# Hybrid decoder trunk: the value projection moved behind scores and softmax, the attention transposes moved inside the output projection

## The chip, the cores and the metric

One core of a Trainium2 chip runs the whole program, one launch. A core has five engines that this text names by their short names: PE (TensorE, matrix products and transposes), DVE (VectorE), ACT (ScalarE), POOL (GpSimd) and SP (SyncE, which here only issues the weight loads). They run side by side and wait for each other through semaphores; each takes its own instructions in order. The metric is the device time of one execution in microseconds (us); the smaller the better. The time before is 628.68 us, the median of 3 runs (627.68 to 630.69).

## The reference

Two layers over 256 tokens of width 1024, all in float32. Cut to what matters here (the mixture of experts behind it is not touched):

```python
for l in range(DEPTH):                                   # DEPTH = 2
    mod = (c_act @ w_ada[l] + b_ada[l])[:, None, :]      # 6 * 1024 wide
    shift1, scale1, gate1, shift2, scale2, gate2 = jnp.split(mod, 6, axis=-1)
    h = rmsnorm(x, norm1_g[l]) * (1.0 + scale1) + shift1
    u = h @ w_in[l]                                      # 1024 x 3072
    u_b, u_c, u_h, u_q, u_k, u_v = jnp.split(u, split_at, axis=-1)
    y_conv = u_b * conv3(u_c * u_h)                      # causal, depthwise, 3 taps
    q = rope(rmsnorm(heads(u_q), q_norm_g[l]), positions)
    k = rope(rmsnorm(heads(u_k), k_norm_g[l]), positions)
    v = heads(u_v)                                       # 8 heads of 64
    y_att = softmax(mask(q @ k.T * scale)) @ v           # one block of 256: plain causal
    y_mix = concat([rmsnorm(y_conv, conv_out_g[l]), rmsnorm(y_att, attn_out_g[l])])
    x = x + gate1 * (y_mix @ w_out[l])                   # 1024 x 1024
    h2 = rmsnorm(x, norm2_g[l]) * (1.0 + scale2) + shift2
    x = x + gate2 * hier_moe(h2, ...)                    # 16 experts, top 2 of one group
```

## The kernel before, in words

Tokens lie in T = 2 tiles of 128 (or, transposed, channels on the partitions and S = 256 tokens in the free dimension). The six blocks of 512 columns of `w_in` and the eight row tiles of `w_out` are multiplied in three passes: ACT writes the rounded weight into `whi` (line 490, `split_half` on ACT), DVE writes the rest `raw - whi` into `wlo` (line 758), and PE adds whi*act_hi, wlo*act_hi and whi*act_lo. A half is 1024 columns of such a pair. A layer has 32 halves: 0 to 11 are q, k and v (three blocks interleaved in two parts), 12 to 15, 16 to 19 and 20 to 23 the blocks B, C and h of the conv, 24 to 31 `w_out`. A half's slot is one of RING = 6, so ACT may not begin half n before PE has used half n-6 (`unit_used`).

Weights come in units of 1 MB into ten slots of `raw` through SP's queue, strictly in the order of the list `stream`: in a layer the 12 units of `w_in` (the first ones earlier), 8 units G (`w_ada` columns of the two gates), 4 units of `w_out`, 8 units M (`w_ada` columns of the second modulation), in layer 0 8 units A (the next layer's first modulation), then the experts. Each unit takes the slot of the unit ten places ahead of it in the list and waits until that one is used up: with the units of a layer's `w_in` and `w_out` counted w0 to w15, G7 waits until w9 (halves 18 and 19) is split, w12 and w13 (the first of `w_out`) until w10 and w11 (halves 20 to 23) are, and the last two of M until w12 and w13 (halves 24 to 27) are.

The order on every engine is written out by hand. In layer l PE does halves 0 to 11 (line 1291, by token), B and C (`conv_block`, line 1307, by channel), transposes q and k (line 1320), h, then attention: `scores` (1344) for pairs of heads u = 0 and 1, the first half of G (1206), `scores(2)`, `probs_T` (1352), the rest of G, `values` (1361 to 1363), and so on pair by pair; then the sum of squares of the conv output (1386), M (1206), the first four row tiles of `w_out` (1396), `ada_cols` (1229), the transposes of the attention rows (1412), and the last four row tiles. DVE squares and sums q and k for their norm (899, 901), applies rope (909 to 922), multiplies C by h (930), does `softmax_max` per pair (939, 944: scale and mask, then a maximum for each token tile), the three taps (972, 974), `heads_out` (953, 956), the conv output's norm (984 to 991) and the attention rows' norm (997 to 1004). ACT takes projections out of PSUM (567, 578, 585, 590, 596), does exp (606), `pT_out` (614) and the square of the conv output (628). POOL only brings the gate rows to all partitions.

PSUM has eight banks; the four pairs of heads use banks 0-1, 4-5, 2-3 and again 0-1 (`PAIR_BANK`), the scores in columns 0 to 383 and the values' result in columns 384 to 511 of the same bank.

## Time and profile before

| what | before |
|---|---|
| median of 3 runs | 628.68 us |
| profiled execution: its own time | 629.93 us |
| its span | 628.1 us |
| mean granted TensorE clock | 0.949 |
| PE busy | 553.2 us (88%) |
| DVE busy | 282.7 us (45%) |
| ACT busy | 218.8 us (35%) |
| bytes moved | 189.77 MB, mean 302 GB/s |

How to read it: the span is the time from the first to the last recorded instruction; the profiled execution took 1.83 us more around it and 1.25 us more than the median. PE is busy most of the time, so idle time of PE and stretches at a low granted clock are what can be gained or lost; the other engines count where PE waits for them. Line numbers (L1307) are those of the kernel before; in the changed kernel they differ by a few.

### The profile page before, as it was taken

What the parts mean: (1) busy time and instruction counts of PE and PEld (TensorE: products, weight loads), DVE (VectorE), ACT (ScalarE), POOL (GpSimd) and SP (SyncE); (2) the same over time, 40 slices, a digit from 0 to 9 for tenths busy, and PEclk for the clock granted to TensorE, in tenths of its full rate; (3) what the DMA queues carried; (4) which work ended last, traced back from release to release, by engine and by line L of the source; (5) the groups of instructions that cost most, each with busy time, mean ns of one, the idle gap of its engine ahead of it and who ended that gap; (6) DMA issues with size and microseconds to landing.
All of it is one profiled execution on the core that took longest, in us unless ns stands there. A gap on an engine that the chain in (4) does not pass through costs nothing.

```text
span 628.1 us, 7864 instructions
## 1 busy us (share of the span) xinstructions
PE 553.2 (88%) x3140; PEld 355.2 (57%) x3140; DVE 282.7 (45%) x495; ACT 218.8 (35%) x379; POOL 17.0 (3%) x74
## 2 busy tenths in 40 slices
PE   3797999869799999999949999986976899999993
PEld 1566899455656534444327899944664644444331
DVE  4516890964266022222377389196326502222233
ACT  2415533641044422221145453364105432232120
POOL 3004000000000000000000000000000000000000
PEclk9898999979798999999987999997978799999998
DMA  8999943891599999999997644299069089999951
GB/s 312 388 387 369 360 158 129 335 423 47 210 417 411 379 386 416 414 412 415 402 387 290 216 143 160 101 365 410 30 229 373 8 288 380 416 413 413 413 213 69
DMA packets 51726, 189.77 MB, mean 302 GB/s; under 512 B 4618, under 2 KB 4698, under 8 KB 44260
## 3 DMA queue, kind: packets, MB, share of 16 engines
q1 hardware_dynamic: 50464, 185.62, 75.9%
q0 software_dynamic: 896, 2.45, 1.1%
q10 hardware_dynamic: 324, 1.13, 0.5%
q8 instruction: 28, 0.46, 0.3%
q14 instruction: 14, 0.11, 0.0%
HBM read 188.12 MB, written 1.06 MB: 301 GB/s over the span
## 4 chain that ended last, share of the span: by engine, by line
PE 77%; DVE 13%; ACT 5%; issue 2%; DMA 1%; DVEq 0%; SPq 0%; ACTq 0%
PE ps L1492 18%; PE ps L1307 11%; PE ps L1291 11%; PE ps L1518 9%; PE ps L1396 6%; PE ps L1472 6%; PE ps L1532 5%; PE ps L1206 4%; DVE wlo L758 3%; PE ps L1237 1%; DMA raw<-in_w_ada_dram 1%; DVE cbc L974 1%; PE ps L1386 1%; ACT whi L490 1%; ACT work L606 1%
## 5 line engine op out<-in xcount | busy, mean ns | idle before, releaser
L758 DVE TENSOR_TENSOR wlo<-raw,whi 128x1024 fp32r<-128x1024 f32 x64 | 75.0, 1221 | 19.3 <-ACT whi L490 19.1
L490 ACT ACTIVATE whi<-raw 128x1024 fp32r<-128x1024 f32 x64 | 64.8, 1054 | 27.1 <-PE ps L1291 8.7
L1492 PE MATMUL ps<-raw,qkT 128*64 128x512 f32 x256 | 58.3, 597 | 1.6 <-ACT work L709 1.6
L1518 PE MATMUL ps<-raw,work 128*64 128x512 f32 x256 | 58.0, 598 | 0.0
L1492 PE MATMUL ps<-raw,cbc 128*64 128x512 f32 x256 | 57.2, 594 | 0.0
L1147 DVE SCALAR_TENSOR_TENSOR work<-ps,cw,work 128x256 f32<-128x256 f32 x16 | 10.9, 684 | 102.7 <-ACT work L703 102.7
L1206 PE MATMUL ps<-raw,c_rep 128*32 128x512 f32 x384 | 46.0, 616 | 10.8 <-DMA raw<-in_w_ada_dram 10.8
L1307 PE MATMUL ps<-act_hi,whi 128*128 128x256 f32 x192 | 54.5, 284 | 0.0
L1307 PE MATMUL ps<-act_hi,wlo 128*128 128x256 f32 x192 | 54.3, 283 | 0.0
L1307 PE MATMUL ps<-act_lo,whi 128*128 128x256 f32 x192 | 54.3, 283 | 0.0
L1136 DVE TENSOR_TENSOR v_sb<-ps,gates 128x512 f32<-128x512 f32 x32 | 22.1, 691 | 64.6 <-PE ps L1518 64.6
L1291 PE MATMUL ps<-whi,act_hi 128*128 128x512 f32 x96 | 39.9, 416 | 7.3 <-DVE act_lo L861 4.0
L1291 PE MATMUL ps<-whi,act_lo 128*128 128x512 f32 x96 | 39.3, 410 | 0.0
L1291 PE MATMUL ps<-wlo,act_hi 128*128 128x512 f32 x96 | 39.3, 409 | 0.0
L693 ACT ACTIVATE whi<-v_sb 128x512 fp32r<-128x512 f32 x32 | 20.0, 629 | 53.8 <-DVE v_sb L1136 45.4
L1472 PE MATMUL ps<-whi,act_hi 128*128 128x256 f32 x128 | 37.1, 319 | 0.9 <-DVE whi L1087 0.9
L1492 PEld LDWEIGHTS ps<-raw,cbc 128*64 128x64 f32 x256 | 18.0, 137 | 34.8 <-issue 33.7
L1472 PEld LDWEIGHTS ps<-whi,act_hi 128*128 128x128 f32 x128 | 26.4, 206 | 18.9 <-issue 18.9
L1307 PEld LDWEIGHTS ps<-act_hi,wlo 128*128 128x128 f32 x192 | 36.8, 192 | 0.1
L1307 PEld LDWEIGHTS ps<-act_hi,whi 128*128 128x128 f32 x192 | 36.8, 192 | 0.1
L1307 PEld LDWEIGHTS ps<-act_lo,whi 128*128 128x128 f32 x192 | 36.8, 192 | 0.0
L1492 PEld LDWEIGHTS ps<-raw,qkT 128*64 128x64 f32 x256 | 17.3, 137 | 33.1 <-issue 28.0
(227 smaller groups left out, 842.2 us busy)
## 6 DMA issues: line engine op xcount, KB each, us to landing
raw<-in_w_ada_dram SPq DMA_DIRECT2D x40, 1024.0 KB, 8.5
raw<-in_w_gate_dram SPq DMA_DIRECT2D x64, 512.0 KB, 7.6
raw<-in_w_up_dram SPq DMA_DIRECT2D x64, 512.0 KB, 9.5
raw<-in_w_down_dram SPq DMA_DIRECT2D x32, 1024.0 KB, 11.4
raw<-in_w_in_dram SPq DMA_DIRECT2D x24, 1024.0 KB, 14.5
raw<-in_w_ada_dram SPq DMA_DIRECT2D x16, 512.0 KB, 11.7
raw<-in_w_out_dram SPq DMA_DIRECT2D x8, 1024.0 KB, 5.2
gates<-gate_line POOLq DMA_DIRECT2D x2, 1024.0 KB, 6.4
```

The lines of the kernel that those rows point to most:

```text
L490: act.activation(whi[:, slot(n), :], raw[:, r, (i % 2) * 1024:(i % 2 + 1) * 1024], ACT.Copy).then_inc(hi_done, 1)
L693: act.activation(y_hi[:, cols], y_f[:, cols], ACT.Copy).then_inc(yhi_ready, 1)
L758: dve.tensor_tensor(wlo[:, slot(n), :], raw[:, ring_slot[("w", l, i // 2)], (i % 2) * 1024:(i % 2 + 1) * 1024], whi[:, slot(n), :].bitcast ...
L1136: dve.tensor_tensor(y_f[:, cols], ps[:, 2 + n, :], gates[:, 1, cols], ALU.mult).then_inc(yg_ready, 1)
L1206: ins = pe.matmul(ps[32 * i:32 * i + 32, 6, :], c_rep[:, row, :], raw[:, ring_slot[unit], i * 512:(i + 1) * 512], start=(k == 0), stop=(k ...
L1291: ins = pe.matmul(ps[:, bank + t, :], acts[pa][:, k, t * P:(t + 1) * P], w[pw][:, kk * 512:(kk + 1) * 512], start=(k == 0 and p == 0), sto ...
L1307: ins = pe.matmul(ps[:, bank + j // 2, (j % 2) * S:(j % 2 + 1) * S], w[pw][:, kk * 512 + j * P:kk * 512 + (j + 1) * P], acts[pa][:, k, :], ...
L1396: ins = pe.matmul(ps[:, 2 * t + n, :], acts[pa][:, k, t * P:(t + 1) * P], w[pw][:, n * 512:(n + 1) * 512], start=(k == 0 and p == 0), stop ...
L1472: ins = pe.matmul(ps[:, bank, j * S:(j + 1) * S], xn[part][:, t, k * P:(k + 1) * P], sel[:, t, 256 * q:256 * (q + 1)], start=(t == 0 and p ...
L1492: ins = pe.matmul(ps[i * SLOTS:(i + 1) * SLOTS, 0, :], hg[p // 2 % 2][:, k, c0:c0 + SLOTS], ws[i][:, :, kk, :], start=(k == 0), stop=(k == ...
L1518: ins = pe.matmul(ps[i * SLOTS:(i + 1) * SLOTS, 2 + n, :], hidT[:, p % 2, kk, i * SLOTS:(i + 1) * SLOTS], ws[i][:, c0:c0 + 512], start=(kk ...
L1532: ins = pe.matmul(ps[:, 4 + 2 * t + n, :], selT[:, 2 * p + t, :], ys[part][:, n * 512:(n + 1) * 512], start=(p == 0 and part == 0), stop=( ...
```

## The change

Nothing that is computed changes, only its order and where it lies.

- The blocks of `w_in` are taken in another order: q, k and B first (halves 0 to 11; B by channel), then C (12 to 15), h (16 to 19) and last v (20 to 23, by token). The list of loads is the same; only which columns a unit holds differs.
- `scores(0)` and `scores(1)` run before h instead of behind all of `w_in`, their softmax under h; `scores(2)` and `scores(3)` run before v, their softmax under v. `probs_T` stands before the last half of each block.
- All of G is accumulated by PE before the first scores, four units ahead of the q and k transposes and four behind them; DVE adds its bias (`gate_row`) before the first softmax.
- The values of all heads are computed in one go behind v, four heads to a bank (0 and 1); `heads_out` runs twice per layer instead of four times.
- q and k are squared and summed one after the other, each as soon as it is out of PSUM; the splits of single halves are spread between the steps.
- The attention rows are transposed behind the first of the eight row tiles of `w_out` instead of behind the fourth.

```diff
-PAIR_BANK = (0, 4, 2, 0)
+PAIR_BANK = (0, 2, 0, 2)
-    IN_ORDER = (3, 4, 5, 0, 1, 2)
+    IN_ORDER = (3, 4, 0, 1, 2, 5)
 # ACT
                 split(l, 10)
+                (qkT out of PSUM, from banks 0-1 and 2-3)
                 exps(0)
                 exps(1)
+                split(l, 11)
+                split_half(l, 24)
+                pT_out(0)
+                pT_out(1)
+                split_half(l, 25)
+                exps(2)
+                exps(3)
                 split(l, 13)
-                pT_out(0)
-                exps(2)
-                pT_out(1)
                 pT_out(2)
-                exps(3)
-                split(l, 14)
                 pT_out(3)
+                split_half(l, 28)
                 act.wait_ge(yconv_ready, l + 1)
                 act.activation(cb, cc, ACT.Square).then_inc(csq_ready, 1)
+                act.wait_ge(unit_used, n0 + 24)
+                act.activation(v_sb[:, :, :], ps[:, 4:6, :], ACT.Copy).then_inc(proj_evac, 1)
                 act.wait_ge(csum_done, l + 1)
...
 # DVE
+                def head_squares(w):
+                    dve.wait_ge(proj_evac, 5 * l + 1 + w)
+                    cols = slice(w * AW, (w + 1) * AW)
+                    squares = wflat[:, w * 1024:(w + 1) * 1024]
+                    link(dve.tensor_tensor(squares.rearrange("p (t d) -> p t d", t=T), tokmaj[:, :, cols],
+                                           tokmaj[:, :, cols], ALU.mult))
+                    dve.tensor_reduce(stat[:, 4:36].rearrange("p (t w h) -> p w t h", t=T, w=2)[:, w, :, :],
+                                      squares.rearrange("p (t h d) -> p t h d", t=T, d=HD),
+                                      AX.X, ALU.add).then_inc(qk_sum, 1)
+                head_squares(0)
                 split(l, 6)
+                head_squares(1)
                 split(l, 7)
-                split(l, 8)
...
-                def heads_out(u):
+                def heads_out(a):
+                    dve.wait_ge(pv_done, 2 * l + a + 1)
+                    dve.tensor_tensor(
+                        tokmaj[:, :, 256 * a:256 * (a + 1)].rearrange("p t (h d) -> p t h d", d=HD),
+                        ps[:, a, :].rearrange("p (h t d) -> p t h d", t=T, d=HD),
+                        stat[:, 20:36].rearrange("p (t h) -> p t h", t=T)[:, :, 4 * a:4 * a + 4].unsqueeze(3)
+                        .to_broadcast([P, T, 4, HD]), ALU.mult).then_inc(yatt_raw, 1)
+                gate_row(l)
                 softmax_max(0)
                 softmax_max(1)
+                split(l, 11)
+                dve.wait_ge(proj_evac, 5 * l + 4)
+                dve.wait_ge(unit_used, n0 + 20)
+                dve.tensor_tensor(cg[:, :, 2:S + 2], cc, ps[:, 4:6, :]..., ALU.mult).then_inc(gated_done, 1)
+                split(l, 12)
                 softmax_max(2)
-                split(l, 13)
+                softmax_max(3)
                 (the three taps, times cb: yconv_ready)
+                split(l, 13)
+                split_half(l, 28)
...
 # PE
+                pe.wait_ge(proj_evac, 5 * l + 1)
+                for half in range(4):
+                    in_half(12 + half, 4, 2 * half, True)
+                ada_acc("G", l, range(0, 4))
+                pe.wait_ge(rope_done, T * (l + 1))
+                qk_transposes(0)
+                qk_transposes(1)
+                ada_acc("G", l, range(4, 8))
                 pe.wait_ge(qkT_ready, 2 * l + 2)
                 scores(0)
                 scores(1)
-                ada_acc("G", l, range(0, 4))
-                pe.wait_ge(gated_done, l + 1)
-                scores(2)
+                pe.wait_ge(proj_evac, 5 * l + 4)
+                for half in range(3):
+                    in_half(16 + half, 4, 2 * half, True)
                 probs_T(0)
                 probs_T(1)
+                in_half(19, 4, 6, True)
+                pe.wait_ge(pT_ready, 4 * l + 1)
+                scores(2)
+                pe.wait_ge(pT_ready, 4 * l + 2)
+                scores(3)
+                pe.wait_ge(gated_done, l + 1)
+                for half in range(3):
+                    in_half(20 + half, 4, 2 * half, False)
+                probs_T(2)
+                probs_T(3)
+                in_half(23, 4, 6, False)
+                (sum of squares of the conv output, into bank 7)
+                pe.wait_ge(pT_ready, 4 * (l + 1))
+                pe.wait_ge(proj_evac, 5 * (l + 1))
                 values(0)
                 values(1)
                 ada_acc("M", l, range(0, 8))
...
                 for half in range(4):
                     for t in range(T):
                         ins = out_half(0, half, t, (0, 1))
                     ins.then_inc(unit_used, 1)
-                ada_cols("M", l)
-                pe.wait_ge(yatt_ready, l + 1)
-                (the 8 transposes of the attention rows)
+                    if half == 0:
+                        ada_cols("M", l)
+                        pe.wait_ge(yatt_ready, l + 1)
+                        (the 8 transposes of the attention rows)
```

How the instructions stand now. First PE around the first scores of layer 0. In the kernel before, the scores of the first two pairs (L1344) stand behind the last matmul of block h (L1307), and the first half of G (L1206, `ps<-raw,c_rep`) behind them:

```order
L1307 MATMUL ps<-act_lo,whi 128x256
L1344 MATMUL ps<-qkT 128x128
L1344 MATMUL ps<-qkT 128x256
L1344 MATMUL ps<-qkT 128x128
L1344 MATMUL ps<-qkT 128x256
L1344 MATMUL ps<-qkT 128x128
L1344 MATMUL ps<-qkT 128x256
L1344 MATMUL ps<-qkT 128x128
L1344 MATMUL ps<-qkT 128x256
L1206 MATMUL ps<-raw,c_rep 32x512 x16
L1344 MATMUL ps<-qkT 128x128
```

In the changed kernel both halves of G (L1208) stand ahead of the scores (L1333), one on each side of the q and k transposes (L1319), and block h begins behind the scores (L1283):

```order
L1208 MATMUL ps<-raw,c_rep 32x512 x16
L1319 MATMUL ps<-ident,tokmaj 128x128 x16
L1208 MATMUL ps<-raw,c_rep 32x512 x16
L1333 MATMUL ps<-qkT 128x128
L1333 MATMUL ps<-qkT 128x256
L1333 MATMUL ps<-qkT 128x128
L1333 MATMUL ps<-qkT 128x256
L1333 MATMUL ps<-qkT 128x128
L1333 MATMUL ps<-qkT 128x256
L1333 MATMUL ps<-qkT 128x128
L1333 MATMUL ps<-qkT 128x256
L1283 MATMUL ps<-act_hi,whi 128x256
```

Moved: the scores of two pairs went from behind block h to ahead of it, and both halves of G to ahead of them.

Second, DVE from the splits before rope to rope, layer 0. Before, both squares and one sum stand behind eight splits (L758), and four more splits stand ahead of rope (L906, L909):

```order
L758 TENSOR_TENSOR wlo<-raw,whi 128x1024 x8
L899 TENSOR_TENSOR work<-tokmaj 128x1024 x2
L901 TENSOR_REDUCE stat<-work 128x32
L758 TENSOR_TENSOR wlo<-raw,whi 128x1024 x4
L906 RECIPROCAL stat<-stat 128x32
L909 TENSOR_TENSOR tokmaj<-tokmaj,stat 128x1024
```

After, q's square and sum (L902, L904) come two splits earlier, and only two splits stand ahead of rope (L913, L916):

```order
L760 TENSOR_TENSOR wlo<-raw,whi 128x1024 x6
L902 TENSOR_TENSOR work<-tokmaj 128x1024
L904 TENSOR_REDUCE stat<-work 128x2x8
L760 TENSOR_TENSOR wlo<-raw,whi 128x1024 x2
L902 TENSOR_TENSOR work<-tokmaj 128x1024
L904 TENSOR_REDUCE stat<-work 128x2x8
L760 TENSOR_TENSOR wlo<-raw,whi 128x1024 x2
L913 RECIPROCAL stat<-stat 128x32
L916 TENSOR_TENSOR tokmaj<-tokmaj,stat 128x1024
```

Moved: q's square and sum went two splits up, and two splits went from ahead of rope to behind its first token tile.

Third, PE in the output projection, layer 0. Before, all four row tiles (L1396) stand ahead of `ada_cols` (L1229) and the attention transposes (L1412):

```order
L1396 MATMUL ps<-whi,act_hi 128x512 x2
L1396 MATMUL ps<-wlo,act_hi 128x512 x2
L1396 MATMUL ps<-whi,act_lo 128x512 x2
L1229 MATMUL ps<-rowsel,mod_rows 128x4 x4
L1412 MATMUL ps<-ident,tokmaj 128x128 x8
L1396 MATMUL ps<-whi,act_hi 128x512 x2
L1396 MATMUL ps<-wlo,act_hi 128x512 x2
```

After, these two (L1231, L1415) stand behind the first row tile, with three row tiles (L1398) behind them:

```order
L1398 MATMUL ps<-whi,act_hi 128x512 x2
L1398 MATMUL ps<-wlo,act_hi 128x512 x2
L1398 MATMUL ps<-whi,act_lo 128x512 x2
L1231 MATMUL ps<-rowsel,mod_rows 128x4 x4
L1415 MATMUL ps<-ident,tokmaj 128x128 x8
L1398 MATMUL ps<-whi,act_hi 128x512 x2
L1398 MATMUL ps<-wlo,act_hi 128x512 x2
```

Moved: 36 projection matmuls now stand between the transposes and the first matmul that needs their result.

## Rows read from the trace of the kernel before

**Rows 1.** Stretches: their length, busy us of PE, PEld, DVE, ACT, POOL, PEclk, DMA, GB/s
```profile
72.10:165.30 93.20, 81.01 (x608) 65.39 (x607) 59.38 (x91) 37.65 (x68) 1.13 (x2) 0.96 0.53 206
369.40:462.50 93.10, 80.81 (x609) 65.23 (x608) 59.46 (x91) 37.65 (x68) 1.13 (x2) 0.96 0.50 195
90.00:92.00 2.00, 2.00 (x19) 2.00 (x18) 2.00 (x2) 0.52 (x1) 0.00 (x0) 1.00 0.00 0
108.90:127.00 18.10, 15.28 (x137) 8.67 (x138) 16.60 (x28) 9.57 (x29) 0.00 (x0) 1.00 0.82 324
127.00:134.00 7.00, 2.73 (x22) 2.05 (x18) 6.83 (x15) 4.23 (x11) 0.56 (x1) 0.96 1.01 420
134.00:141.00 7.00, 5.79 (x24) 5.00 (x28) 2.43 (x2) 2.92 (x4) 0.56 (x1) 0.56 1.02 419
165.30:174.00 8.70, 8.67 (x27) 6.90 (x28) 0.19 (x1) 0.00 (x0) 0.00 (x0) 0.68 0.99 417
188.00:300.00 112.00, 109.35 (x578) 54.37 (x572) 30.03 (x69) 35.13 (x68) 1.05 (x2) 0.98 1.01 405
```

**Rows 2.** Chain of waits, layer 0, 72 to 182: start us, us, what
```profile
72.08 23.05 PE ps L1307 x192
...
135.22 3.78 PE ps L1386 x8
...
140.48 0.22 PE ps L1362 x2
...
140.93 7.00 PE ps L1206 x64
147.93 11.15 PE ps L1396 x48
159.08 1.65 PE ps L1229 x8
...
165.33 8.39 PE ps L1396 x24
```

**Rows 3.** Timeline of PE: start us, us, line, operation, count, idle before
```profile
108.76 1.69 PE L1344 MATMUL ps<-qkT 64*128 64x128 f32 x16
110.38 3.64 PE L1206 MATMUL ps<-raw,c_rep 128*32 128x512 f32 x32
...
116.29 0.88 PE L1352 MATMUL ps<-ident,work 128*128 128x128 f32 x6 [1.41 <-ACT work L606]
...
160.58 1.07 PE L1412 MATMUL ps<-ident,tokmaj 128*128 128x128 f32 x8
```

**Rows 4.** Timeline of DVE, layer 0
```profile
67.80 2.48 DVE L899 TENSOR_TENSOR work<-tokmaj 128x1024 f32<-128x1024 f32 x2 [2.13 <-ACT tokmaj L567]
70.32 2.29 DVE L901 TENSOR_REDUCE stat<-work 128x32 f32<-128x2048 f32 x1
72.52 4.62 DVE L758 TENSOR_TENSOR wlo<-raw,whi 128x1024 fp32r<-128x1024 f32 x4
...
89.96 4.63 DVE L758 TENSOR_TENSOR wlo<-raw,whi 128x1024 fp32r<-128x1024 f32 x4
...
112.35 0.95 DVE L939 SCALAR_TENSOR_TENSOR work<-ps,mask 128x768 f32<-128x768 f32 x1
113.33 1.01 DVE L944 TENSOR_REDUCE stat<-work 128x2 f32<-128x256 f32 x2
...
121.79 1.00 DVE L974 SCALAR_TENSOR_TENSOR cbc<-cg,mix_col,cbc 128x256 f32<-128x256 f32 x2
...
147.51 0.88 DVE L1004 TENSOR_SCALAR tokmaj<-tokmaj,stat 128x512 f32<-128x512 f32 x2
```

**Rows 5.** Timeline of ACT: the square of the conv output
```profile
134.12 1.05 ACT L628 ACTIVATE cbc<-cbc 128x1024 f32<-128x1024 f32 x1
```

**Rows 6.** Timeline of SP's queue, 80 to 93: the last gate unit
```profile
84.95 0.37 SPq L331 DMA_DIRECT2D raw<-in_w_ada_dram  x1
```

**Rows 7.** Page, part 6: DMA issues, KB each, us to landing
```profile
raw<-in_w_out_dram SPq DMA_DIRECT2D x8, 1024.0 KB, 5.2
```

More of the change, by code:

```diff
@@ L615, in pT_out @@
                                    ACT.Copy).then_inc(pT_ready, 1)
+                split(l, 4)
+                split(l, 5)
+                qk_out(0)
+                split(l, 6)
+                qk_out(1)
+                split(l, 7)
+                act.wait_ge(qk_sum, 2 * (l + 1))
+                act.activation(stat[:, 4:36], stat[:, 4:36], ACT.Sqrt, scale=1.0 / HD,
+                               bias=eps_col).then_inc(qk_root, 1)
+                act.wait_ge(unit_used, n0 + 12)
+                act.activation(cb, ps[:, 2:4, :].rearrange("p a (b s) -> p (a b) s", s=S),
+                               ACT.Copy).then_inc(proj_evac, 1)
@@ new lines, in _ @@
+                split(l, 8)
+                split(l, 9)
+                act.wait_ge(unit_used, n0 + 16)
+                act.activation(cc, ps[:, 4:6, :].rearrange("p a (b s) -> p (a b) s", s=S),
+                               ACT.Copy).then_inc(proj_evac, 1)
+                split(l, 10)
+                act.wait_ge(rw_ready, 1)
+                for w in range(2):
+                    act.wait_ge(qkT_done, 2 * l + w + 1)
+                    bank = (0, 2)[w]
+                    act.activation(qkT[:, w, :, :],
+                                   ps[:, bank:bank + 2, :].rearrange("p a (b s) -> p (a b) s", s=S),
+                                   ACT.Copy).then_inc(qkT_ready, 1)
@@ L992, in _ @@
                                   ALU.subtract).then_inc(ymc_ready, 1)
-                heads_out(3)
-                dve.wait_ge(yatt_raw, 4 * (l + 1))
+                for a in range(2):
+                    heads_out(a)
+                dve.wait_ge(yatt_raw, 2 * (l + 1))
                 for t in range(T):
```

196 lines of the change are left out of this document (63 added, 133 removed).

## The prediction

> **What bounds the kernel now.** I read the stretches first, then the chain of waits, then the timelines of single engines inside the stretch that the chain shows to be weak.
>
> The stretch that the change rewrites runs from the start of half 12 (72.1) to the start of the last four row tiles of `w_out` (165.3): 93.2 us in layer 0 and 93.1 in layer 1 [rows 1]. PE is busy for 81.0 of them, so 12.2 us per layer are waits, and part of the busy time is slow. The reader is to see two holes in it. From 127 to 134 PE works 2.73 of 7 us while DVE works 6.83, and in the next 7 us the granted clock is 0.56, that is, mostly at 1.2 of 2.4 GHz; the four sums of squares took 3.78 us there [rows 1, 2]. And behind the attention transposes, which end at 161.65, PE starts again only at 165.33; its first 24 records then take 8.39 us where 48 of the same kind took 11.15, so 2.8 us more than at the full clock, the clock being 0.68 over that stretch [rows 1 to 3]. The engine in front of PE is DVE (16.60 of 18.10 us busy from 108.9 to 127), not the DMA queues (share 0.53 over the stretch) [rows 1].
>
> Outside this stretch the order of work stays as it is, except that the four halves of B (by channel) and of v (by token) change places. 23.05 us for eight halves by channel is 2.88 each [rows 2]; I take the other kind as equal, since both stream the same 6,144 columns.
>
> **PE's work in the stretch, from rows.** Twelve halves 34.6 (12 x 2.88, [rows 2]); G 7.3 (2 x 3.64), scores 3.4 (2 x 1.69), `probs_T` 3.5 (4 x 0.88), q and k transposes 2.1 and attention transposes 1.1 (1.07 for eight) [rows 3]; sum of squares 1.9 (half of 3.78, since at the full clock), values 5.3 (4 pairs x 6 x 0.22), M 7.0, four row tiles 11.15, `ada_cols` 1.65 [rows 2]. Sum 79.0. The change neither adds nor removes PE work; what it can remove is the other 14.2 us of 93.2, and the 2.8 us behind it.
>
> **The new order, replayed for layer 0.** I lay PE's work end to end and, at each wait, ask when the other engine gets there.
>
> - Halves 12 to 15 end at 83.6, G0 to G3 at 87.3. The transposes need rope. Before, rope ends and the next splits begin at 89.96. Now two splits (half of 4.62) stand behind the first part of rope instead of ahead of it, and q's half of square and sum (half of 2.48 + 2.29) runs earlier, where DVE had waited 2.13 us for ACT [rows 4]. So rope ends at about 89.96 - 2.3 - 2.4 = 85.3: covered. Transposes end at 89.4, G4 to G6 at 92.1.
> - G7 is the first new wait. Its slot is freed by the split of w9, which stands directly behind rope: 85.3 + 2.3 = 87.6. Before, G7 was issued at 84.95 [rows 6] and DMA had fallen silent by 90 [rows 1], so it lands within 5.1 us; units of `w_out`, equally alone, took 5.2 [rows 7]. G7 lands at 92.8: a wait of 0.7, PE at 93.6. Queued behind it are the scores on PE and `gate_row` on DVE, and behind that both maxima and the split of w11. Scores end at 95.3.
> - Halves 16 to 18 run to 103.9. Under them lie two rounds of scale, mask and maximum (1.96 each, [rows 4]), from 94.5 to 98.4, and the exps, so `probs_T` starts at once; 105.7. Half 19 to 108.6, scores 2 and 3 to 110.3.
> - Now DVE runs for its money. From 108.6: C times h 1.24, splits 2.3, two maxima 3.9, taps 5.7 (4 x 1.43), times cb 1.24, that is 14.4 us, then ACT's square 1.05 [rows 4, 5]: 124.1. PE needs scores, halves 20 to 22, two `probs_T` and half 23: 15.0, 123.6. A wait of 0.5. The sum of squares ends at 126.0, values at 131.3, M at 138.3.
> - The normed conv output must be there by 138.3, 12.3 us behind the sum of squares; before, the row tiles started at 147.93, 8.9 us behind it, without a wait for DVE [rows 2]. Covered.
> - First row tile 141.1, `ada_cols` 142.8. The attention rows were ready at 148.4 before, 9.4 us behind the sum of squares (135.22 + 3.78) [rows 2, 4]. One more split and the remaining heads (about 1.9) make it 137.3. Covered by 5.5 us. Transposes 143.8.
> - Three row tiles, 8.4 us, lie where PE waited 3.7 us: the second half starts at 152.2 and, with no hole ahead of it, at the full clock.
>
> Gain per layer: 165.3 - 152.2 = 13.1, plus 2.8 for the clock, less 0.3 for some seven hand-offs of 0.04 that the replay leaves out: 15.6. Layer 1 has the same stretch within 0.1 us and the same waits, so 31.2 in all. The profiled execution would fall from 629.93 to 598.7 (its span from 628.1 to 596.9, with 1.83 around it); the median of the runs lies 1.25 below it, 628.68 - 31.2 = 597.5. I say 598.
>
> **Edits that cost nothing, and what hides them.** `gate_row` earlier: 0.7 us on DVE, ahead of maxima that have 5 us to spare under halves 16 to 18. The M units: w13 waits for the split of w11, now at 103.3 instead of 94.6; it and the ten units behind it follow at 2.5 us each (1.05 MB at 420 GB/s, [rows 1]), M7 at 133.5, needed at 137.4. That leaves 3.9 us; beyond it every us is lost. Two `heads_out` instead of four save little on DVE, off the path. The experts begin earlier as a whole and their loads with them; PE is busy 109.35 of 112 us there beside a DMA share of 1.01 [rows 1], so they neither gain nor lose, unless PE meets units that are not there yet: the loads of A and of the experts start at the split of w15, just ahead of the second half of `w_out`, and that half gets 2.8 us shorter. So a loss of 0 to 2.8 us per layer; I take 0, since PE was 98% busy there and waited for none of them.
>
> **Where the skill's pages speak.** By the stretch of 90 to 92 and by 5.2 us to landing, a lone unit is there some 5 us after its issue [rows 1, 7]. The Trainium skill, "DMA: Bandwidth & Descriptors", section Bandwidth, gives 6.15 us of DMA time for 1 MB in one transfer. By that G7 would come at 93.8 or later, 1.0 us later per layer, and the time would be 600; by the rows it is 598. From 108.9 to 127 PE waited for up to 1.41 us at a time and was granted 1.00 throughout [rows 1, 3]; after the hole from 127 to 134 it got 0.56. The skill's "TensorE: Matmul & The Clock Gate" (The HAM clock gate) says that "the default state is throttled, and activity releases the throttle", and that its window runs freely. By it even the two short waits left could now and then cost a slow piece: half of 3.78 us is what one such piece cost here, 1.9 per layer, 602 in all; by the row on 108.9 to 127, nothing.
>
> **The rivals.**
> - The helpers become the bound. DVE's 14.4 + 1.05 us against PE's 15.0 is a tie, and ACT must fit exps, splits and `pT_out` between in a fixed order. If two splits of ACT and one exp (1.05 + 1.05 + about 1.9) come to lie on that path, and PE's wait grows to 4.5 us, the clock falls behind it (1.9): 5.9 per layer, 597.5 + 11.8 = 609. For it: DVE already has 16.60 busy of 18.10 us from 108.9 to 127. Against: ACT's share there is 9.57.
> - The attention chain stays late. If the attention rows miss the transposes by more than the 5.5 us of cover, the old hole comes back, 3.7 + 2.8 per layer, with up to 3 more ahead of it: 597.5 + 2 x 9.5 = 616. Against: the 5.5 us.
> - M comes late, and the kernel is slower. SP's queue is in order, w13 stands behind the split of w11, and that now stands behind two maxima, `gate_row` and so G7. One mechanism, priced at 1 us per us from 107.2 on (103.3 + 3.9), and it eats the whole gain of 15.6 at about 123. If the split of w11 slipped to 124.5, behind the second pair of maxima, the time would be 628.7 + 2 x 1.7 = 632. Against: everything that it waits for is over by 102.3 in the replay.
> - The change moves the waits and doesn't remove them: the v block takes the place of h in front of the values, and something equally long waits for it. 628 to 629. Against: in the replay v's copy ends 0.9 us before the sum of squares does.
>
> **How the numbers follow.** Forecast (594 to 604) 0.62, helpers (604 to 612) 0.20, attention chain (612 to 625) 0.10, no change 0.04, slower 0.04. Less than 594 would need waits under 0 in the replay, so the lower end is short; on the upper side I go to 612, which leaves out some 0.18. What can be told from no change is about 0.5%, 3.1 us: faster 0.92, same 0.04, slower 0.04.
>
> **What would show it.** Half 12 to the second half of `w_out` lasts about 80 us instead of 93 in both layers, with PE busy for 79; granted clock close to 1.00 over it and no 8.4 us for 24 records behind it; one wait under 1.5 us on a G unit ahead of the scores, and one near the square of the conv output. I am wrong if PE waits more than 3 us at any single place of this stretch, if M7 is what it waits for, or if the stretch of the experts grows.

## The result and the profile after

The changed kernel takes 593.72 us (median of 4 runs, 593.09 to 599.98) against 629.60 us of the kernel before on the same chip: a ratio of 0.946, with a 95% interval of 0.943 to 0.950. Six more runs in another group gave 594.62 to 601.41 with a median of 596.89 (experiment 9), a ratio of 0.950 (0.947 to 0.954). The forecast was 598.0. The profiled execution took 593.54 us (its span 591.7) where the one before took 629.93 (628.1).

The page of the changed kernel, first its span, then busy time, then the granted clock in 40 slices:

```profile
span 591.7 us, 7838 instructions
...
PE 537.3 (91%) x3140; PEld 344.2 (58%) x3140; DVE 281.3 (48%) x479; ACT 219.2 (37%) x379; POOL 17.0 (3%) x74
...
PEclk9899999999999999999988999999996999999998
```

The stretch that the change rewrites, from the start of half 12 to the second half of `w_out`, now has these two rows, one per layer (columns as in [rows 1]: length, busy us of PE, PEld, DVE, ACT and POOL, granted clock, DMA share, GB/s):

```profile
70.60:150.10 79.50, 77.61 (x563) 61.33 (x562) 56.24 (x80) 37.65 (x67) 1.13 (x2) 1.00 0.66 254
349.00:428.70 79.70, 77.59 (x563) 61.32 (x562) 56.25 (x80) 37.65 (x67) 1.13 (x2) 1.00 0.61 232
```

They answer to the first two of [rows 1]: 93.20 and 93.10 us became 79.50 and 79.70, PE stands idle for 1.9 and 2.1 us instead of 12.2 and 12.3, and the clock is 1.00 throughout. What PE still waits for in layer 0 is this (in total, times, longest, us):

```profile
PE ps L1385 <- ACT cbc L626: 1.4, 1, 1.4
PE ps L1208 <- DMA raw<-in_w_ada_dram: 0.5, 1, 0.5
```

The chain that ended last, layer 0 (start us, us, what), which answers to [rows 2]:

```profile
83.73 2.37 DVE wlo L760 x2
86.12 4.83 DMA raw<-in_w_ada_dram
90.99 1.07 PE ps L1208 x8
92.06 1.61 PE ps L1333 x16
93.67 8.83 PE ps L1283 x72
102.50 1.31 PE ps L1341 x12
103.81 2.88 PE ps L1283 x24
106.78 1.22 DVE cg L963
...
119.73 1.24 DVE cbc L976
120.98 1.06 ACT cbc L626
122.09 1.99 PE ps L1385 x8
129.39 7.00 PE ps L1208 x64
136.40 2.95 PE ps L1398 x12
139.35 1.64 PE ps L1231 x8
140.99 0.93 PE ps L1415 x8
141.92 13.66 PE ps L1398 x60
```

Two places are to be seen. From 83.73 to 90.99 the chain runs through DVE's splits and the load of G7; from 106.78 to 122.09 it leaves PE for DVE and ACT. And the last line is one piece: 60 projection matmuls without a hole, where before 24 of them stood alone behind a wait of 3.7 us. The last 24 of the 60 take 5.5 us (at 0.227 us each), against 8.39 in the kernel before.

**Where 36.4 us went** (628.1 to 591.7). The stretch lost 13.7 us in layer 0 and 13.4 in layer 1. The 24 matmuls behind it lost 2.9 and 2.8. Sum 32.8. The other 3.6 us lie outside the rewritten stretches: 1.5 ahead of half 12 in layer 0, 1.3 at the start of the experts of layer 0, 1.0 in the first twelve halves of layer 1, and 0.2 given back elsewhere. At each of these three places the kernel before has a piece at the low clock level (54.5 to 58.5, 194.5 to 198.5 and 335 to 338 us) that the profile of the changed kernel lacks. Experiment 9 shows that such pieces come and go in one and the same kernel. Over the experts behind the first of these pieces the distance between the two traces stays at 19.3 to 19.4 us, so they neither gained nor lost, as forecast.

One part of the exchange is not clock. B by channel now stands outside the stretch and v by token inside it, and a half by channel takes 2.88 us where one by token takes 2.72 to 2.75. In layer 1, at full clock, the four halves of B cost 0.6 us more than the four of v that stood there, and the stretch is 0.5 us shorter for the same reason. Of the 13.4 to 13.7 us that the stretch lost, this half microsecond is moved and not won.

### The profile page after: what moved, and what is told of

Read it like the earlier page. It is cut to its first block, busy times and chain, and to the rows that moved or that the text cites. A ratio compares the mean times of both kernels' runs of the same rounds, so it can differ in the third digit from the quotient of the medians.

```text
span 591.7 us, 7838 instructions
## 1 busy us (share of the span) xinstructions
PE 537.3 (91%) x3140; PEld 344.2 (58%) x3140; DVE 281.3 (48%) x479; ACT 219.2 (37%) x379; POOL 17.0 (3%) x74
## 4 chain that ended last, share of the span: by engine, by line
PE 72%; DVE 17%; ACT 3%; DMA 3%; issue 2%; DVEq 0%; SPq 0%; ACTq 0%
PE ps L1496 19%; PE ps L1522 10%; PE ps L1290 8%; PE ps L1476 6%; PE ps L1398 6%; PE ps L1283 5%; PE ps L1536 5%; PE ps L1208 5%; DVE wlo L760 4%; DMA raw<-in_w_ada_dram 3%; DVE work L921 2%; PE ps L1239 1%; DVE cbc L974 1%; DVE tokmaj L916 1%; DVE res L1020 1%
## 5 line engine op out<-in xcount | busy, mean ns | idle before, releaser
L490 ACT ACTIVATE whi<-raw 128x1024 fp32r<-128x1024 f32 x64 | 65.0, 1056 | 29.7 <-PE ps L1283 14.3
L1208 PE MATMUL ps<-raw,c_rep 128*32 128x512 f32 x384 | 46.3, 615 | 11.7 <-DMA raw<-in_w_ada_dram 11.7
L1283 PE MATMUL ps<-act_hi,whi 128*128 128x256 f32 x192 | 54.9, 286 | 0.0
L1283 PE MATMUL ps<-act_hi,wlo 128*128 128x256 f32 x192 | 54.3, 283 | 0.0
L1283 PE MATMUL ps<-act_lo,whi 128*128 128x256 f32 x192 | 54.3, 283 | 0.0
L1290 PE MATMUL ps<-whi,act_hi 128*128 128x512 f32 x96 | 39.5, 411 | 7.2 <-DVE act_lo L863 3.9
L1290 PE MATMUL ps<-wlo,act_hi 128*128 128x512 f32 x96 | 38.6, 402 | 0.0
L1290 PE MATMUL ps<-whi,act_lo 128*128 128x512 f32 x96 | 38.4, 400 | 0.0
L1283 PEld LDWEIGHTS ps<-act_hi,whi 128*128 128x128 f32 x192 | 36.8, 192 | 1.6 <-issue 1.5
L1283 PEld LDWEIGHTS ps<-act_hi,wlo 128*128 128x128 f32 x192 | 36.8, 192 | 0.1
L1283 PEld LDWEIGHTS ps<-act_lo,whi 128*128 128x128 f32 x192 | 36.8, 192 | 0.0
L1476 PE MATMUL ps<-whi,act_hi 128*128 128x256 f32 x128 | 35.7, 311 | 0.9 <-DVE whi L1089 0.9
L1476 PEld LDWEIGHTS ps<-whi,act_hi 128*128 128x128 f32 x128 | 25.3, 198 | 18.9 <-issue 18.9
```

What stands on the lines that cost most here:

```text
L490: act.activation(whi[:, slot(n), :], raw[:, r, (i % 2) * 1024:(i % 2 + 1) * 1024], ACT.Copy).then_inc(hi_done, 1)
L1208: ins = pe.matmul(ps[32 * i:32 * i + 32, 6, :], c_rep[:, row, :], raw[:, ring_slot[unit], i * 512:(i + 1) * 512], start=(k == 0), stop=(k ...
L1283: ins = pe.matmul(ps[:, bank + j // 2, (j % 2) * S:(j % 2 + 1) * S], w[pw][:, kk * 512 + j * P:kk * 512 + (j + 1) * P], acts[pa][:, k, :], ...
L1290: ins = pe.matmul(ps[:, bank + t, :], acts[pa][:, k, t * P:(t + 1) * P], w[pw][:, kk * 512:(kk + 1) * 512], start=(k == 0 and p == 0), sto ...
L1476: ins = pe.matmul(ps[:, bank, j * S:(j + 1) * S], xn[part][:, t, k * P:(k + 1) * P], sel[:, t, 256 * q:256 * (q + 1)], start=(t == 0 and p ...
```

## The experiments

The kernel before took 628.5 to 628.7 us in each group of runs below. The stretch is always the one above; for the changed kernel it is 79.5 and 79.7 us. The changed kernel had 593.7 us in its first group and 596.9 in a later one (experiment 9), so a difference of a few us between medians is not told from noise, and the small edits are judged by their stretches.

**1. The attention transposes back behind all four row tiles**, the rest of the change kept.

```diff
-                    if half == 0:
+                    if half == 3:
                         ada_cols("M", l)
                         pe.wait_ge(yatt_ready, l + 1)
```

> The changed kernel with one part undone: the attention transposes and ada_cols again behind the fourth row tile of w_out. Theory (the prediction's sum: the hole of 3.7 us behind the transposes and 2.8 us of low clock after it were the price of their old place): both come back in each layer, so 2 x 6.5 = 13 us more than the changed kernel's 593.7, about 606.5, and the first 24 records of the second half take about 8.4 us again. Rival 1 (the gain came from attention alone; DVE and ACT are now early enough that the hole stays closed): 594. Rival 2 (the hole comes back but the denser work ahead keeps the clock up): 2 x 3.7 = 601.

Measured: 607.16 us (606.75 to 609.56), ratio 0.967 (0.963 to 0.972). The hole is back, as the timeline of PE has it (start, us; in brackets the idle time ahead and what ended it):

```profile
153.48 1.22 PE L1398 MATMUL ps<-whi,act_hi 128*128 128x512 f32 x2 [3.65 <-DVE act_lo L1012]
```

and the chain of waits says what it costs behind it:

```profile
148.91 0.94 PE ps L1415 x8
150.25 1.21 ACT work L640 x3
151.48 0.70 DVE act_hi L1011
152.20 1.24 DVE act_lo L1012
153.48 7.70 PE ps L1398 x24
```

The same 24 matmuls take 7.70 us, 2.2 more than without the hole. The medians alone (10.3 us above experiment 9's 596.9, 13.4 above the 593.7 of the first group) don't decide between 13 us and the 7.4 of a hole without low clock; the traces do: stretch and 24 matmuls together are 5.9 us longer in layer 0 and 6.5 in layer 1, of which 2.2 and 2.6 are the slow matmuls. Cause and place are shown.

**2. The transposes alone**: the kernel before, with `ada_cols` and the attention transposes behind the first row tile.

```diff
                     ins.then_inc(unit_used, 1)
-                ada_cols("M", l)
-                pe.wait_ge(yatt_ready, l + 1)
...
+                    if half == 0:
+                        ada_cols("M", l)
+                        pe.wait_ge(yatt_ready, l + 1)
```

> The kernel before with this one part alone: transposes and ada_cols behind the first row tile. Theory: 13 us less than before's 629.6, about 617, since the chain transposes, copy, cast and subtraction (3.7 us) now lies beside 8.4 us of row tiles; ACT's split of the last half stands in front of the copy and costs up to 2.8 us of that cover, not of the time. With e1 it says whether the two parts add up: 13 + 23 = 36. Rival (the split in front of the copy makes the copy late, the hole stays): 625 or more.

Measured: 617.19 us (615.97 to 617.69), ratio 0.982 (0.977 to 0.986). Alone this edit is worth 11.5 us; behind the new order it is worth 607.16 - 596.89 = 10.3 (experiments 1 and 9), and the new order without it 628.66 - 607.16 = 21.5. Alone they make 33.0, together 31.7: the two parts add up within what the medians tell, and neither covers the other. The waits for the h block and for the sum of squares are still there: in the chain of this kernel L1386 takes 3.78 us as in [rows 2], and L1396 x60 takes 13.66.

**3. The hole filled**: the kernel before, with seven matmuls of 256 columns that nothing reads behind the transposes. It keeps the wait and takes away only the idleness.

```diff
                 ins.then_inc(yT_done, 1)
+                for i in range(7):
+                    pe.matmul(ps[:, 6, 0:256], ones[:, :], mask[:, 0:256], start=True, stop=True)
```

> The kernel before with seven extra matmuls (ones times the mask, 256 columns, into the PSUM bank that ada_cols has just freed; their result is not used) behind the attention transposes, some 3.5 us of PE work in the hole of 3.7 us. It prices the clock alone. Theory (the low clock of the second half of w_out comes from PE's hole ahead of it): the hole stays as long, the 24 records take 5.5 instead of 8.4 us, 2 x 2.8 us less, about 624. Rival 1 (the low clock has another cause): 629.6. Rival 2 (the extra matmuls delay the second half): above 630.

Measured: 625.14 us (621.11 to 626.96, 10 runs), ratio 0.993 (0.990 to 0.995). The chain has the 24 matmuls behind the hole, 5.77 us instead of 8.39:

```profile
164.68 1.23 DVE act_lo L1011
165.96 5.77 PE ps L1396 x24
```

So the 2.8 us per layer that the prediction put down to the clock behind the hole are clock, and not data that came late: the second half starts no earlier (165.96 against 165.33), and the same matmuls are fast. The medians fell by 3.5 us and not by 5.6: in the profiled execution, the slowest of the ten, the low piece behind PE's wait of 2.8 us for ACT's exps in layer 1 lasts from 424 to 438 us, twice as long as in the kernel before, and that stretch is 2.1 us longer.

**4. The squares of q and k joined again** (changed kernel), which was to make rope and the split that frees G7's slot come later.

```diff
-                head_squares(0)
                 split(l, 6)
+                head_squares(0)
                 head_squares(1)
```

> The changed kernel with DVE's squares and sums of q and k again together, behind the split of halves 12 and 13. Theory (G7's load is the last thing ahead of the scores, and its slot is freed by the split behind rope): rope ends 2.4 us later, G7 lands 2.4 us later, PE's wait for it grows from 0.5 to 2.9 us, and every us of it is a us of the time: 2 x 2.4 = 4.8 more, 598.5, perhaps 1.5 per layer more where the clock falls. Rival (rope has cover and the softmax has room to catch up under halves 16 to 18): 594.

Measured: 600.78 us (597.77 to 601.44), but not for the reason expected. The wait for G7 is only 0.8 us in layer 0 and 1.1 in layer 1, the stretches last 79.7 and 80.1: 0.6 us together, not 4.8. DVE had stood idle around the first square (1.31 us ahead of it, 0.69 ahead of the second, in layer 0 of the changed kernel); with the squares joined the split fills that time, and rope ends 0.2 us later, counted from the start of the stretch, instead of 2.4. The rest of the 7 us above 593.7 (4 above 596.9) lies outside the stretch, where pieces at the low clock level are longer (by span and mean granted clock 25.2 us of clock are missing, against 15.4 and 19.7 in the two profiles of the changed kernel); experiment 9 bears on them. The size in the expectation was wrong.

**5. G4 to G7 behind the scores** (changed kernel), so that PE has work while G7 lands. The expectation speaks of the last gate unit alone; the edit moves all four.

```diff
-                ada_acc("G", l, range(4, 8))
                 pe.wait_ge(qkT_ready, 2 * l + 2)
                 scores(0)
                 scores(1)
+                ada_acc("G", l, range(4, 8))
```

(`gate_row(l)` on DVE moves behind the second maximum.)

> Against the changed kernel: the last gate unit of ada_acc (the eight matmuls that wait for a 1 MB load, 0.53 us in layer 0 and 0.74 us in layer 1) stands behind the scores of heads 0 and 1 instead of ahead of them, so the scores run while the load lands. Theory that this wait is the price of the early gate unit: both waits vanish and the stretches shorten by 0.5 and 0.7 us, 593.7 to about 592.5. Rival, that something behind it (the sum of squares, which waits for the conv weight blocks' squares) was late anyway: the wait there grows from 1.4 us to about 2 us and the time stays 593.7. Read from the waits and the stretches, since 1 us is below what the time alone tells.

Measured: 600.40 us (598.13 to 602.84). The stretches last 80.0 and 80.0 us, so this edit loses 0.5 and 0.3. The waits of the stretch in layer 0:

```profile
PE ps L1385 <- ACT cbc L626: 1.4, 1, 1.4
PE ps L1333 <- ACT qkT L609: 1.2, 1, 1.2
```

The wait for the load is gone and a longer one took its place: the scores (L1333) now follow the transposes at once and wait for ACT's copy of them. G4 to G6 had hidden that copy, which nothing in the profile of the changed kernel shows, because a hidden wait has no row. Neither side of the expectation was right. G7 alone behind the scores, with G4 to G6 (2.8 us) left as cover for the copy, was not tried, so whether the 0.5 and 0.7 us can be had that way stays open.

**6. Two units of M ahead of the sum of squares** (changed kernel): 16 matmuls where PE waits 1.4 us.

```diff
+                ada_acc("M", l, range(0, 2))
                 pe.wait_ge(csq_ready, l + 1)
...
-                ada_acc("M", l, range(0, 8))
+                ada_acc("M", l, range(2, 8))
```

> Against the changed kernel: two of the eight units of M (16 of 64 matmuls, 1.75 us) stand ahead of the sum of squares, on which TensorE waits 1.4 us in each layer for VectorE and ScalarE. Theory: the wait is filled, 1.4 x 2 = 2.8 us less, 593.7 to about 590.9. Rival, that the norm and output projection behind it are ready later than TensorE then is: the wait comes back before the half of w_out, or at the units' loads, and the time stays 593.7.

Measured: 596.30 us (593.26 to 598.20). The chain of layer 0 no longer leaves PE between the scores and the end of the stretch:

```profile
118.73 2.75 PE ps L1290 x12
121.48 1.85 PE ps L1208 x16
123.34 1.93 PE ps L1386 x8
130.56 5.29 PE ps L1208 x48
```

The stretches last 78.0 and 78.8 us, 1.5 and 0.9 less; in layer 1 a longer wait for G7 (1.1 instead of 0.7) took part of it back. The gain of 2.4 is shown in the stretches and not in the times: it is smaller than what the clock pieces elsewhere move them by.

**7. Less work on DVE ahead of the sum of squares** (changed kernel without one of the three convolution taps).

```diff
-                    for k in (1, 2):
+                    for k in (2,):
```

> The changed kernel without one of its three convolution taps (that part of the computation is left out), which takes about 2 us of VectorE's work in each layer ahead of the sum of squares and nothing of TensorE's. Theory, that VectorE has cover everywhere in the stretch but at the sum of squares: its 1.4 us wait vanishes in both layers, 2.8 us less, about 590.9, and no more than that. Rival, that VectorE bounds the stretch (the case of 609 in the prediction): 2 us or more per layer, 589.7 or less. Rival, that the wait is for ScalarE alone: 593.7.

Measured: 597.50 us (592.38 to 597.81), stretches of 78.5 and 79.3 us. The wait at the sum of squares, layer 0:

```profile
PE ps L1385 <- ACT cbc L626: 0.5, 1, 0.5
```

Taking 2 us from DVE brings 0.9 at this place. The reason why it is not 1.4 lies with ACT. In the changed kernel it stood idle for 0.75 us ahead of the square (first row, timeline of ACT); here its own splits and copies reach up to the square (chain of this run; start, us):

```profile
120.98 1.06 ACT L626 ACTIVATE cbc<-cbc 128x1024 f32<-128x1024 f32 x1 [0.75 <-DVE cbc L976]
```

```profile
117.41 1.89 ACT whi L490 x2
119.90 0.79 ACT work L584
120.69 0.94 ACT whi L490
121.64 0.96 ACT cbc L626
```

So DVE was the last to arrive by less than 1 us. If DVE bounded the stretch, it would be shorter by the full 2 us per layer; it is shorter by 1.0 and 0.4. Experiment 6 speaks for both helpers together: nothing is taken from either, and once PE has other work ahead of the sum of squares its wait there is gone. Speeding up one of the two alone soon stops paying.

**8. The slower rival, forced** (changed kernel): the splits of blocks 11 and 12 behind the last softmax maximum, so that SP's queue stands.

```diff
                 softmax_max(3)
+                split(l, 11)
+                split(l, 12)
```

(and not at their places ahead of the conv block's product and of the maxima.)

> The changed kernel with the splits of weight blocks 11 and 12 on VectorE put behind the softmax maximum of the last head, so their buffers come free later and SyncE issues the loads queued behind them later, those of M among them. It is the prediction's rival that ended slower, forced. Theory: the split of block 11 ends at 116.4 instead of 102.1, so block 13 and all behind it in SyncE's queue are issued 14.3 us later; the last unit of M then lands at about 146.6 where TensorE wants it at 135.5, 11 us in each layer, about 615. Rival, that SyncE's queue has slack enough (M is 16 x 256 KB pieces that were issued long ahead): 593.7 to 596.

Measured: 619.74 us (616.62 to 623.12), ratio 0.986 (0.980 to 0.991). The queue of SP in this kernel (start, us, line, how many issues), and then in the changed kernel:

```profile
88.38 27.17 SPq L339 DMA_DIRECT2D raw<-in_w_out_dram  x4
115.59 22.61 SPq L331 DMA_DIRECT2D raw<-in_w_ada_dram  x9
```

```profile
88.39 15.17 SPq L339 DMA_DIRECT2D raw<-in_w_out_dram  x4
103.61 46.70 SPq L331 DMA_DIRECT2D raw<-in_w_ada_dram  x15
```

The four issues of `w_out` end 12.0 us later, the M units behind them too (eight loads of 1 MB, not the sixteen small ones of the expectation), and the chain has the wait:

```profile
125.55 20.05 DMA raw<-in_w_ada_dram
145.64 1.94 PE ps L1208 x8
147.58 4.83 PE ps L1398 x12
```

M7 is there at 145.6 (146.6 expected). The stretches last 92.5 and 93.1 us, 13.0 and 13.4 more. In layer 0 PE begins M7 10.1 us later than in the changed kernel, and the other 2.9 us are low clock behind its waits: the eight matmuls of M7 take 1.94 us instead of 0.87, the twelve of the first row tile 4.83 instead of 2.95. PE's wait at the sum of squares grew too, from 1.4 to 3.9 us, because ACT's split ahead of the square had to wait 5.5 us for a unit of `w_out`; that costs nothing more, since PE would have waited for M7 instead. The split of block 11 ends at 114.1 here and at 102.1 in the changed kernel, 12.0 us apart as the queue is (the expectation took 14.3, which is the end of block 12). So the mechanism of the prediction's slower rival is real, and dearer than it was priced. By the prediction's slack of 3.9 us and 1 us per us, 12.0 us would cost 8.1; the slack is 1.9 (see below), and the clock adds 2.9: 13.0. Even so the kernel is not slower than the one before.

**9. The changed kernel once more.**

> The changed kernel, with nothing altered, on another day and perhaps another chip, to see how far its own time moves. Its four times so far are 593.1, 593.5, 593.9 and 600.0 with a mean granted clock of 0.977, 0.974, 0.974 and 0.958. Theory: the same program falls into several patterns of stretches at the low clock level, mostly behind the idle time at the layer boundary (304 to 316 us) and around the routing (444 to 460 us); its times spread from 593 to 600 again and go with the granted clock. Rival, that 600 was a stray: all times 593 to 594.5.

Measured: 596.89 us (594.62 to 601.41, 6 runs, granted clock 0.970 down to 0.958). The stretches of its profiled execution last 79.5 and 79.9 us, as before, yet it took 597.58 us, 4.0 more than the first. The stretches of 4 us from 50 on show one such place, here first in this execution, then in the first one:

```profile
50.00:54.00 4.00, 0.94 (x4) 0.84 (x5) 3.97 (x12) 4.00 (x6) 3.20 (x7) 1.00 1.08 356
54.00:58.00 4.00, 4.00 (x12) 3.11 (x12) 4.00 (x5) 0.99 (x2) 0.00 (x0) 0.57 1.06 348
```

```profile
50.00:54.00 4.00, 0.70 (x6) 0.53 (x6) 3.93 (x13) 4.00 (x6) 4.00 (x8) 1.00 1.07 357
54.00:58.00 4.00, 4.00 (x18) 3.33 (x19) 4.00 (x4) 1.82 (x2) 0.02 (x1) 1.00 1.07 354
```

PE did nearly nothing from 50 to 54 in both, with one idle spell of 3.3 us. Behind it the clock was 0.57 in one (12 matmuls done in 4 us) and 1.00 in the other (18). The same program, the same idle time, a different outcome. The place is the same in all 14 profiles of this study: the low piece follows in 11 of them, and is missing in the first one of the changed kernel and in those of experiments 1 and 12. By span and mean granted clock, the clock time missing is 19.7 us here (595.8 us at 0.967) and 15.4 in the first execution (591.7 at 0.974); the difference, 4.3, is about the 4.0 us between the two. In both executions such pieces lie behind idle spells (22 to 26, 303 to 311, 440 to 444) or at the very end; this one has a further piece from 177 to 181, ahead of which PE was busy for 3.0 of 4 us. What decides whether one comes was not found out.

**10 and 11. The idle time at the layer boundary filled** with 16 matmuls of 256 columns (10), and that together with experiment 6 (11).

```diff
                 if l > 0:
+                    for i in range(16):
+                        pe.matmul(ps[:, 0, 0:256], ones[:, :], mask[:, 0:256], start=True, stop=True)
                     transposes(2 * l)
```

> The changed kernel with 16 matmuls of 256 columns added (about 6 us of work that nothing reads) ahead of the transposes at the layer boundary, where TensorE otherwise stands idle for 7.9 us and the clock is at its low level from 304 to 316 us (to 326 us in other kernels of this study). Theory that this idle time brings the slow stretch: it vanishes, the 16 transposes take about 2.4 instead of 3.7 us and the first halves of layer 1 run at full clock, 1 to 5 us less than the unchanged kernel on the same chip. Rival, that the slow stretch comes on its own schedule: it stays, and the added work costs nothing to 2 us.

> Both edits together: two units of M ahead of the sum of squares, and the filled layer boundary. The first shortened the two stretches by 1.5 and 0.9 us, the second is expected to give 1 to 5 us: 3.4 to 7 us less than the unchanged changed kernel on the same chip, about 588 to 592 if that one is at 595.

Measured: 602.08 us (599.04 to 604.92) and 598.77 (598.34 to 599.49), where the unchanged one had 596.89. Experiment 10 is slower; 11 can't be told from the unchanged one, whose times span 594.6 to 601.4. The gain that the theory promised didn't come. The timeline of PE in 10:

```profile
312.65 9.10 PE L1275 MATMUL ps<-mask,ones 128*128 128x256 f32 x32 [6.08 <-issue]
```

Of the 7.86 us that PE seems to wait for DVE, it can't work in the first 6.08. `issue` means that it waited for nothing the profile shows. In the code only the jump over the branch for overflowing experts (a value loaded into a register, a comparison, a branch that isn't taken) lies between the last scatter and this place, so I put the 6.1 us down to it; it was not measured by itself. The added matmuls began when only 1.8 us were left, took 9.1 us instead of the 6 that I had allowed, and the idle spell ahead of the low clock stayed:

```profile
308.00:312.00 4.00, 0.00 (x0) 0.00 (x0) 3.82 (x4) 0.34 (x1) 0.00 (x0) 0.72 1.05 386
312.00:316.00 4.00, 3.35 (x8) 2.75 (x9) 3.15 (x8) 0.59 (x2) 0.00 (x0) 0.50 1.06 388
```

From the last scatter to the first half of layer 1 it is 20.7 us now instead of 14.7. Whether a filled boundary would keep the clock up is therefore not shown: it couldn't be filled. Experiment 11 against 10 isolates the edit of experiment 6 once more: 3.3 us less, and stretches of 78.2 and 78.2 us against 79.5 and 79.5.

**12. Three gaps around the last layer's router filled too**, with four matmuls each.

```diff
+                if l + 1 == L:
+                    for i in range(4):
+                        pe.matmul(ps[:, 6, 0:256], ones[:, :], mask[:, 0:256], start=True, stop=True)
                 pe.wait_ge(asg_ready, l + 1)
```

(and the same ahead of the transposes and between their two token tiles)

> As the combination, and in the last layer four matmuls of 256 columns (1.5 us each group) more in each of three gaps around the routing: ahead of the transposes, between their two halves, and ahead of the placement matmuls, where the clock is at its low level from 444 to 460 us. Theory, the same as for the layer boundary: that stretch vanishes or shortens too, 2 to 4 us less than the combination. Rival, that the gaps are too short of cover or the added matmuls delay what is behind them: equal to the combination, or up to 2 us more.

Measured: 598.10 us (596.84 to 599.07) against 598.77 of experiment 11. One row each, of 11 and then of 12, from the end of layer 1's output projection to the first matmul of the experts on the routed rows:

```profile
445.20:466.10 20.90, 13.15 (x76) 10.61 (x76) 13.54 (x38) 9.31 (x15) 0.00 (x0) 0.76 0.51 208
```

```profile
445.00:463.90 18.90, 14.82 (x101) 11.56 (x99) 13.55 (x38) 9.31 (x15) 0.00 (x0) 1.00 0.59 239
```

The low pieces at 450 to 454 and 457 to 464 are gone, and the same way takes 2.0 us less although PE has 25 more records in it, with DVE and ACT as busy as before. In these two executions the theory holds, at the lower end of its 2 to 4 us. The medians differ by 0.7 us only: the mean granted clock of the five executions of 12 is 0.983 in two and 0.977 in three, against 0.974 in all five of 11, and the two sets of times overlap.

No version here beats the changed kernel beyond what can be told. The edit of experiment 6 shortens its stretches by 2.4 us, and is the one that I would keep.

## Why the prediction was right

- **The terms.** 31.2 us were forecast, 15.6 per layer: 13.1 for the stretch, 2.8 for the clock behind it, less 0.3. The trace has 13.7 and 13.4 for the stretch and 2.9 and 2.8 for the clock, 32.8 in all. Experiments 1 and 3 show that the latter belong to the hole.
- **PE's work as the floor.** 79.0 us had been summed from rows; PE is busy for 77.6. The surplus is two terms: a half by token was taken as 2.88 us like one by channel and takes 2.75 (L1290 x12 in the chain of experiment 6), 0.5 us per layer, a choice that had no row of its own, and no gain of the program, since the halves of B now cost as much more outside; and `probs_T` was summed one pair at a time (0.88 each), where two pairs together take 1.31 (L1341), 0.9 us per layer.
- **The wait for G7.** Predicted 0.7, measured 0.53 and 0.74. In layer 0 everything lies some 1.5 us earlier than in the replay, because the stretch begins at 70.6 and not at 72.1: rope ends at 83.7 (85.3), G7 is issued at 86.12 (87.6), PE comes at 90.5 (92.1). Counted from the start of the stretch the replay had these three times right within 0.1 us.
- **The skill's figure for the load.** From issue to landing it took 4.83 and 5.04 us in the chain, as the rows on lone units had it (5.2 [rows 7]); by the 6.15 us of the Trainium skill, "DMA: Bandwidth & Descriptors" (Bandwidth), which that page gives for loads that GpSimd issues and not for SP's queue, the wait would have been some 1.2 us longer. The measurement decides for the rows.
- **The wait at the sum of squares.** Predicted 0.5, measured 1.4 in both layers. PE came 1.4 us earlier than in the replay, counted from the start of the stretch, by the same two terms (halves by token and `probs_T`), DVE and ACT only 0.5. This is the wait that was mis-sized, 0.9 us per layer; the time doesn't show it, because PE's work was smaller by more. Experiments 6 and 7 show that it is one wait at one place: filled with other work it goes altogether, and with 2 us less of DVE's work it falls to 0.5. That this error and the one in PE's work (0.9 too little, 1.4 too much) largely cancel is luck; the length of the stretch alone doesn't show them.
- **The covers.** The attention rows were ready at 135.0 and used at 141.0, a cover of 6.0 where 5.5 was forecast. M came in time, but by less than forecast: its last unit was issued at 123.2 us and landed 10.2 us later, at 133.4, and PE reached it at 135.4, so 1.9 us of cover and not 3.9. Counted from the start of the stretch it landed 1.4 us later than in the replay, and PE was there 0.6 us earlier. Experiment 8 shows what it costs when M is late: 1 us per us, and the low clock behind the waits on top, which the prediction's price left out.
- **The clock inside the stretch.** 1.00 in both layers, as by the row on 108.9 to 127 [rows 1]. The rule of the Trainium skill, "TensorE: Matmul & The Clock Gate" (The HAM clock gate), as the prediction read it, by which even short waits could cost a slow piece, would have given 602. Waits of 0.4 to 1.4 us brought none in ten profiles (the changed kernel, twice, and experiments 1, 4, 5, 6, 7, 10, 11 and 12; in 6, 11 and 12 only the wait for G7 is left, and in 1 this holds up to the hole behind the transposes). In experiment 8, with single waits of up to 3.9 us, there were pieces at 124 to 128 and 144 to 152.
- **What the forecast left out.** It took the rest of the program as fixed. The rest moved by 3.6 us in the profiled pair and by a few us between executions of one kernel. The distance between 598.0 and 593.7 is 1.6 us of terms and, for the larger part, this; against the median of the six later runs, 596.9, it is 1.1 us. "Less than 594 would need waits under 0 in the replay" was the weak step: 593.7 came with waits of 1.9 us per layer, because PE's work in the stretch was 1.4 us smaller than summed and the clock outside it was kinder. The range needed a few us more below the sum for that alone; that the first group lies 0.3 us below 594 and the later one 2.9 above it is the chance of the clock pieces.

## What to carry to other kernels

Sum the work of the bounding engine over a stretch from rows, and take it as the floor; then replay the new order and look at every wait between. What can be gained is idle time, plus the slow matmuls that can stand behind an idle spell of 3 us or more (behind the holes of 3.7 us here they stood in all four cases, behind one of 3.3 us in 11 of 14). A unit of work that depends on nothing is worth most where it covers a wait, and before it is moved one must ask what it covers now, since a covered wait has no row (experiment 5). And where one program's own executions differ by 1%, judge edits of 1 to 3 us by the length of the stretch they touch.

## What the runs showed of the hardware that was not expected

- Behind the same idle spell of 3.3 us the clock falls in one execution and not in another (0.57 and 1.00 from 54 to 58 us; it fell in 11 of 14 profiles). The changed kernel's ten runs spread from 593.1 to 601.4 us, and the mean granted clock with them from 0.977 to 0.958.
- An apparent wait can hold time in which the engine couldn't have worked. 6.1 of 7.9 us at the layer boundary could not be filled, with nothing in the code there but the jump over a body that isn't run.
- A matmul of 256 columns on fp32 operands that are not rounded took 0.46 us in experiment 3 (3.19 us for seven, 14 records) and 0.57 in experiment 10 (9.10 us for 16, 32 records, at a clock that was low for part of it). On the rounded halves of `w_in` one of 256 columns takes 0.12 us (24 in 2.88).
- Work that nothing reads can pay: with it, in experiment 12, the clock of the router's stretch was 1.00 instead of 0.76, and the stretch took 18.9 us instead of 20.9. In the medians (598.77 and 598.10) that can't be told.
